# Four modulation units move to TensorE and the third piece is added whole

## The chip, the cores and the metric

The kernel runs on one core of a Trainium2 chip. The metric is the device time of one execution in microseconds. The kernel before takes 972.9 us (median of 3 runs, 971.4 to 973.92).

## The reference

Two layers of a decoder trunk on 256 tokens of width 2048, all in float32. Each layer computes a modulation from the conditioning vector `c`, scales and shifts the normalised input with it, and multiplies the result by a wide input projection:

```
c_act = silu(c)
for l in range(DEPTH):
    mod = c_act @ ada_w[l] + ada_b[l]              # (2048) @ (2048 x 6144)
    shift, scl, gate_res = split(mod, 3)
    h = _rms(x, norm_g[l]) * (1.0 + scl) + shift   # (256 x 2048)
    z = h @ w_in                                   # first layer: 2048 x 6144
    ...                                            # pooling and attention, or sparse attention and convolution
    x = x + gate_res * ((y * silu(g)) @ w_out[l])
```

What matters here is the start of the first layer: `c_act @ ada_w[0]` for the first 4096 of its columns (scale and shift), `h`, and the first twelve blocks of 128 columns of `z`.

## The kernel before, in words

**Modulation.** The weights `ada_w` come in *units* of 128 x 1024 float32 (512 KB). Sixteen units make a *piece*, which gives 1024 values of the modulation. Four pieces (units 0 to 63) hold scale and shift of the first layer, each for four of the sixteen 128-wide chunks of `h`. VectorE adds a unit into `acc` as unit times one column of `cact` plus `acc` (`add_units`, L1242). When a piece is complete, TensorE sums `acc` over the partitions: for each of 8 blocks of 128 columns one product of the block with a column of ones, written to one column of a bank (`reduce_part`, L948). VectorE adds the bias (L1266), makes the gain (L1279) and scales `X` (L1315); ScalarE adds the shift (L535). Then `h` of the chunk is there.

**Halves.** A piece can also be added in column halves: the first 8 units hold all rows of the first 512 columns, the other 8 those of the last 512. The first two chunks of the four need only the first half. In the kernel before the third and the fourth piece go so (`halved`, `half_units`, L1259 and L1262: two adds of 128 x 512 for a unit). For the fourth piece the host has put the units in this order; for the third the load itself picks the halves out of two units (`load_halves`, L334), in rows of 2 KB instead of 4 KB.

**The wide stage.** The first twelve blocks of `z` are multiplied by TensorE at once, in twelve half banks. Their weights come in twelve *wide slabs* of 1 MB and sixteen tiles. Chunk `c` of `h` is multiplied by tiles 12c to 12c + 11 (`unsplit_chunk`, L914: twelve float32 products 128 x 128 by 128 x 256, each of which the trace shows as two records). After chunk 15 ScalarE evicts the banks (L672), and the kernel goes on slab by slab to its end.

**Order.** It is written out by hand on each engine. SP issues all loads in one queue in program order: units, and wide slabs between them. A unit's load waits until its slot is free (a ring of 12), so until the unit 12 before has been added (`ada_done`); slab i waits for TensorE to have finished slab i - 4 (`pe_half`), and all behind it in SP's queue wait too. TensorE runs the chunks in order; ahead of some stand the sums: both halves of piece 0 before chunk 0 and of piece 1 before chunk 4, then the first half of piece 2 before chunk 7 and the second before chunk 9, the first half of piece 3 before chunk 11 and the second before chunk 14. Small products with the identity (`keep_warm`, L844) fill some waits.

Of the kernel before, what the change touches and what calls it, by code (L numbers as in the profile page):

```python
# [11 lines left out]
P = 128  # L12
D_MODEL = 2048
SEQ = 256
# [25 lines left out]
PIECE = 1024  # L40
# [16 lines left out]
RING = 12  # L57
TILES = KC

# [47 lines left out]
def build(nc, xT, params, pool_w, w_slabs, ada_units, x1_dram, outT):  # L107
    ctx = ExitStack()
    with ctx:
# [3 lines left out]
        def sem(name):  # L113
            return ctx.enter_context(nc.semaphore(name))
# [70 lines left out]
        half_sum = sem("half_sum")  # L185
        mod_done = sem("mod_done")
# [55 lines left out]
        def unit_slot(n):  # L242

            return n % RING if n < FIRST else n % 4
# [71 lines left out]
        def _(sp):  # L316
            sp.sem_inc(lo_done, 4 + 2 * UNSPLIT)
            sp.sem_inc(ada_done, 4)
            sp.dma_start(par[:], params).then_inc(par_in, 16)
            def load_units(n, count, t):  # L320
                for u in range(count):
                    unit = n + u if t is None else n + u + 4 * t
                    if n >= FIRST:
                        sp.wait_ge(ada_done, unit + 1)
                    elif unit >= RING:
                        sp.wait_ge(ada_done, unit - RING + 5)
# [3 lines left out]
            def load_halves(p, first, last):  # L330
                for n in range(first, last):
                    unit, half, u = UNITS * p + n, n // 8, n % 8
                    sp.wait_ge(ada_done, unit - RING + 5)
                    sp.dma_start(unit_at(unit).rearrange("p (a n) -> p a n", a=2),  # L334
                                 ada_units[UNITS * p + 2 * u:UNITS * p + 2 * u + 2, :,
                                           PIECE // 2 * half:PIECE // 2 * (half + 1)]
                                 .rearrange("a p n -> p a n")).then_inc(ada_in[unit_slot(unit)], 16)
# [498 lines left out]
        def _(pe):  # L836
# [70 lines left out]
            def unsplit_chunk(c):  # L907

                pe.wait_ge(h_done, c + 1)
                for s in range(WIDE[0]):  # L910
                    i, k = (WIDE[0] * c + s) // TILES, (WIDE[0] * c + s) % TILES
# [167 lines left out]
            halved = (2, 3)  # L1079

            def reduce_half(p, half):
                pe.wait_ge(ada_done, UNITS * p + 8 * (half + 1) + 4 if p in halved else UNITS * (p + 1) + 4)
                if not half and p:
                    pe.wait_ge(mod_done, p)
                for j in range(4 * half, 4 * half + 4):
                    ins = reduce_part(p, j, half=True)
                if not half:
                    ins.then_inc(half_sum, 1)

            for c in range(12):  # L1090
                p = c // GROUP
                if c % GROUP == 0 and p not in halved:
                    if p:
                        warm_until(UNITS + 13, UNITS + 15)
                    else:
                        warm_until(11, 15)
                    reduce_half(p, 0)
                    reduce_half(p, 1)
                if c % GROUP == GROUP - 1 and p + 1 in halved:
                    reduce_half(p + 1, 0)  # L1100
                if c % GROUP == 1 and p in halved:
                    reduce_half(p, 1)
                unsplit_chunk(c)
# [114 lines left out]
        def _(dve):  # L1218
# [33 lines left out]
            def half_units(first, count):  # L1252
                for unit in range(first, first + count):
                    u, p, half = unit % UNITS, unit // UNITS, PIECE // 2
# [3 lines left out]
                    dve.wait_ge(ada_done, unit + 4)  # L1258
# [233 lines left out]
            add_units(UNITS, 16, None)  # L1492
# [12 lines left out]
            for j in range(6):  # L1505
                lower_h(0, j)
# [3 lines left out]
            for j in range(6, 14):  # L1510
                lower_h(0, j)
            lower_h(0, 14)
            lower_h(0, 15)
# [313 lines left out]
```

## Time and profile before

| | |
|---|---|
| median of 3 runs | 972.9 us |
| the profiled execution | 975.36 us |
| its span, first to last instruction | 973.6 us |
| TensorE busy | 941.4 us (97%) |
| VectorE busy | 822.2 us (84%) |
| ScalarE busy | 427.5 us (44%) |
| mean DMA rate | 268 GB/s |
| first eviction of the wide stage | 145.46 us into the span |

Busy times of engines overlap, so they don't add up to the span. A busy share is an average over stages: the wide stage covers the first 15% of the span and has other limits than what follows. Times of rows are microseconds from the start of the span.

### The profile page before, as it was taken

How to read it: one execution, taken by the hardware profiler on the slowest of the kernel's cores; microseconds unless marked ns; L12 is line 12 of the kernel's file. 1: busy time of each engine (PE TensorE's matmuls, PEld its weight loads, DVE VectorE, ACT ScalarE, POOL GpSimd, SP SyncE). 2: the span in 40 equal slices, each digit the busy share in tenths (PEclk: the TensorE clock that was granted, in tenths of full speed). 3: DMA queues.
4: the chain of work that ended last, by engine and by line, in shares of the span. 5: the costliest groups of instructions: out<-in, count | busy, mean ns of one | idle time of the engine just before them, and what ended most of it. 6: DMA issues, size and time to landing. Idle time of an engine off the chain costs nothing.

```text
span 973.6 us, 18573 instructions
## 1 busy us (share of the span) xinstructions
PE 941.4 (97%) x7050; PEld 906.1 (93%) x7050; DVE 822.2 (84%) x1244; ACT 427.5 (44%) x742; POOL 92.5 (9%) x100
## 2 busy tenths in 40 slices
PE   4898899999999999999999999999999999999998
PEld 4887789999999999999999999999999999998887
DVE  5887868987889879998888898999999886879963
ACT  3210116444565444434445534444556655743331
POOL 1000000010110000122200000253011100000000
PEclk9999899999999999999999999999999999999999
DMA  9999978888876888899858655544555445698962
GB/s 360 412 402 404 408 267 292 309 328 336 330 275 252 310 281 312 323 352 355 326 205 284 217 190 174 176 146 159 174 173 196 173 167 201 201 308 298 360 226 76
DMA packets 76595, 261.27 MB, mean 268 GB/s; under 512 B 8288, under 2 KB 8928, under 8 KB 74608
## 3 DMA queue, kind: packets, MB, share of 16 engines
q1 hardware_dynamic: 73680, 251.38, 71.7%
q0 software_dynamic: 2848, 8.99, 2.6%
q8 instruction: 43, 0.70, 0.3%
q14 instruction: 24, 0.20, 0.1%
HBM read 256.07 MB, written 4.19 MB: 267 GB/s over the span
## 4 chain that ended last, share of the span: by engine, by line
PE 73%; DVE 20%; DMA 3%; issue 1%; ACT 1%; SPq 0%; DVEq 0%; ACTq 0%
PE bank L857 12%; PE bank L858 12%; PE bank L859 12%; DVE wlo L1232 6%; PE bank L878 6%; DVE Y L1452 6%; PE bank L914 5%; PE bank L1001 4%; PE bank L1003 4%; PE bank L1004 4%; PE bank L876 3%; DMA ada<-ada_units 2%; PE bank L927 2%; PE bank L896 2%; PE bank L902 2%; PE bank L898 2%
## 5 line engine op out<-in xcount | busy, mean ns | idle before, releaser
L517 ACT ACTIVATE whi<-raw 128x1024 fp32r<-128x1024 f32 x258 | 272.1, 1060 | 378.6 <-PE bank L859 206.5
L1232 DVE TENSOR_TENSOR wlo<-raw,whi 128x1024 fp32r<-128x1024 f32 x258 | 313.5, 1232 | 63.5 <-ACT whi L517 62.0
L857 PE MATMUL bank<-hhi,whi 128*128 128x256 f32 x912 | 262.5, 288 | 1.7 <-ACT T L763 0.9
L858 PE MATMUL bank<-hlo,whi 128*128 128x256 f32 x912 | 258.0, 283 | 0.0
L859 PE MATMUL bank<-hhi,wlo 128*128 128x256 f32 x912 | 257.9, 283 | 0.0
L1242 DVE SCALAR_TENSOR_TENSOR acc<-ada,cact,acc 128x1024 f32<-128x1024 f32 x140 | 182.5, 1303 | 22.7 <-DMA ada<-ada_units 12.3
L857 PEld LDWEIGHTS bank<-hhi,whi 128*128 128x128 f32 x912 | 174.9, 192 | 4.5 <-issue 3.1
L858 PEld LDWEIGHTS bank<-hlo,whi 128*128 128x128 f32 x912 | 175.0, 192 | 0.1
L859 PEld LDWEIGHTS bank<-hhi,wlo 128*128 128x128 f32 x912 | 174.8, 192 | 0.0
L1001 PE MATMUL bank<-whi,hhi 128*128 128x256 f32 x512 | 146.7, 287 | 0.0
L1003 PE MATMUL bank<-whi,hlo 128*128 128x256 f32 x512 | 144.8, 283 | 0.0
L1004 PE MATMUL bank<-wlo,hhi 128*128 128x256 f32 x512 | 144.8, 283 | 0.0
L1452 DVE SCALAR_TENSOR_TENSOR Y<-U,par,Y 128x256 f32<-128x256 f32 x240 | 105.2, 504 | 0.0
L1001 PEld LDWEIGHTS bank<-whi,hhi 128*128 128x128 f32 x512 | 98.2, 192 | 0.8 <-issue 0.7
L1003 PEld LDWEIGHTS bank<-whi,hlo 128*128 128x128 f32 x512 | 98.2, 192 | 0.1
L1004 PEld LDWEIGHTS bank<-wlo,hhi 128*128 128x128 f32 x512 | 98.2, 192 | 0.0
L878 PE MATMUL bank<-both_g,whi 128*128 128x512 f32 x256 | 89.5, 398 | 0.0
L857 PE MATMUL bank<-both_g,whi 128*128 128x256 f32 x256 | 73.3, 286 | 0.3 <-DVE both_g L1353 0.3
L858 PE MATMUL bank<-both_g,whi 128*128 128x256 f32 x256 | 72.4, 283 | 0.0
L859 PE MATMUL bank<-both_g,wlo 128*128 128x256 f32 x256 | 72.4, 283 | 0.0
L876 PE MATMUL bank<-both_g,wlo 128*128 128x256 f32 x240 | 68.1, 284 | 0.0
L878 PEld LDWEIGHTS bank<-both_g,whi 128*128 128x128 f32 x256 | 47.2, 188 | 10.2
(197 smaller groups left out, 1296.4 us busy)
## 6 DMA issues: line engine op xcount, KB each, us to landing
raw<-w_slabs SPq DMA_DIRECT2D x258, 512.0 KB, 4.5
ada<-ada_units SPq DMA_DIRECT2D x152, 512.0 KB, 6.6
pre<-ada_units SPq DMA_DIRECT2D x40, 512.0 KB, 15.8
raw<-w_slabs SPq DMA_DIRECT2D x6, 1024.0 KB, 15.9
V<-w_slabs SPq DMA_DIRECT2D x3, 1024.0 KB, 17.7
Y<-w_slabs SPq DMA_DIRECT2D x3, 1024.0 KB, 15.7
X<-xT SPq DMA_DIRECT2D x2, 1024.0 KB, 10.9
x_dram<-X POOLq DMA_DIRECT2D x4, 512.0 KB, 8.2
```

The source lines that it names most:

```text
L517: act.activation(whi[:, slot], raw[:, slot], ACT.Copy).then_inc(hi_done, 1)
L857: mm(out, whi[:, s, k, :], ahi[:, c, :], start=(c == 0), stop=False)
L858: mm(out, whi[:, s, k, :], alo[:, c, :], start=False, stop=False)
L859: last = mm(out, wlo[:, s, k, :], ahi[:, c, :], start=False, stop=(c == KC - 1))
L876: mm(out[:, 0:SEQ], wlo[:, s, k, :], ghi[:, c, :], start=False, stop=False, skip_group_check=True)
L878: last = mm(out[:], whi[:, s, k, :], flat(both_g[:, c]), start=(c == 0), stop=(c == KC - 1), skip_group_check=True)
L1001: mm(out, hhi[:, c, tokens], upper, start=(c == 0 and q == 0), stop=False, skip_group_check=True)
L1003: mm(out, hlo[:, c, tokens], upper, start=False, stop=False, skip_group_check=True)
L1004: last = mm(out, hhi[:, c, tokens], lower, start=False, stop=(c == KC - 1), skip_group_check=True)
L1232: dve.tensor_tensor(wlo[:, s], raw[:, s], whi[:, s].bitcast(F32), ALU.subtract)\
L1242: dve.scalar_tensor_tensor(acc[:, p % 2, :], unit_at(first + u), cact[:, bass.ds(k, 1)], acc[:, p % 2, :], ALU.mult, ALU.add).then_inc(ada ...
L1452: ins = dve.scalar_tensor_tensor(Y[:, j, :], U[:, j, k:k + SEQ], par[:, wcol:wcol + 1], Y[:, j, :], ALU.mult, ALU.add)
```

## The change

The third piece is no longer added in halves but whole, like the first two, and its units are loaded whole. Four units (31, 47, 55 and 63, the last of pieces 1 and 2 and of each half of piece 3) are not added by VectorE: TensorE multiplies each by its column of `cact`, eight products of 128 x 128 by 128 x 1, straight into the columns of the bank in which the sum over `acc` then accumulates. They stand inside chunks 3, 7, 10 and 12 (`unsplit_chunk(c, at, between)`). The sum of piece 2 stands whole between chunks 7 and 8; the half sums of piece 3 stand inside chunks 11 and 13. A new semaphore, `pe_added`, frees the slots of TensorE's units. VectorE makes all low parts of `h` (`lower_h`) at the end.

```diff
+ON_PE = (31, 47, 55, 63)
+def added(unit):
+    return unit - sum(3 * UNITS <= u < unit < FIRST for u in ON_PE)
...
             for i, first, last in ((4, 0, 3), (5, 3, 8), (6, 8, 11), (7, 11, 13), (8, 13, 16)):
-                load_halves(2, first, last)
+                load_units(2 * UNITS + first, last - first, None)
                 load_wide(sp, i)
...
+            def add_unit(unit):
+                p, n = unit // UNITS, unit % UNITS
+                pe.wait_ge(ada_in[unit_slot(unit)], 16 * unit_uses(unit, None))
+                if p < 3:
+                    for j in range(HC):
+                        ins = mm(sums(p, j)[:, j:j + 1], unit_at(unit)[:, j * P:(j + 1) * P], cact[:, n:n + 1],
+                                 start=j == 0 or p < 2 and j == HC // 2, stop=False, skip_group_check=True)
...
+                ins.then_inc(pe_added, 1)
...
+            def reduce_third():
+                pe.wait_ge(ada_done, 3 * UNITS - 1 + 4)
+                for j in range(HC):
+                    ins = reduce_column(2, j)
+                    if j == 0:
+                        ins.then_inc(ada_done, 1)
+                    if j == HC // 2 - 1:
+                        ins.then_inc(half_sum, 1)
+                ins.then_inc(mod_sum, 1)
+                keep_warm(4, M[:, SEQ:SEQ + P])
...
-            unsplit_chunk(12)
-            unsplit_chunk(13)
-            pe.wait_ge(ada_done, UNITS * 4 + 4)
-            for j in range(4, HC):
-                reduce_part(3, j)
-            keep_warm(6, M[:, 0:P])
+            warm_until(11, 15)
+            reduce_whole(0)
+            unsplit_chunk(0)
+            unsplit_chunk(1)
+            unsplit_chunk(2)
+            unsplit_chunk(3, 10, unit_31)
+            reduce_whole(1)
+            unsplit_chunk(4)
+            unsplit_chunk(5)
+            unsplit_chunk(6)
+            unsplit_chunk(7, 9, unit_47)
+            reduce_third()
+            unsplit_chunk(8)
+            unsplit_chunk(9)
+            unsplit_chunk(10, 9, unit_55)
+            unsplit_chunk(11, 7, lambda: reduce_half(3, 0))
+            unsplit_chunk(12, 9, unit_63)
+            unsplit_chunk(13, 9, lambda: reduce_half(3, 1))
             unsplit_chunk(14)
             unsplit_chunk(15)
...
-            half_units(2 * UNITS, 8)
-            half_units(2 * UNITS + 8, 1)
-            first_half(2)
-            half_units(2 * UNITS + 9, 7)
+            add_units(2 * UNITS, 15, None)
             dve.wait_ge(acc_zero, 4)
             half_units(48, 1)
+            dve.wait_ge(mod_sum, 3)
+            first_half(2)
             second_half(2)
```

TensorE's program from the end of chunk 6 to the start of chunk 9, in the kernel before (L914 is a product of a chunk, L948 one of a sum):

```order
L914 MATMUL bank<-X,raw 128x256 [waits wide_in1]
L914 MATMUL bank<-X,raw 128x256 x3
L948 MATMUL bank<-ones,acc 128x1 [waits mod_done,ada_done]
L948 MATMUL bank<-ones,acc 128x1 x3
L914 MATMUL bank<-X,raw 128x256 [waits wide_in1,h_done]
L914 MATMUL bank<-X,raw 128x256 x11
L914 MATMUL bank<-X,V 128x256 [waits wide_in2,h_done]
L914 MATMUL bank<-X,V 128x256 x11
L948 MATMUL bank<-ones,acc 128x1 [waits ada_done]
L948 MATMUL bank<-ones,acc 128x1 x3
L914 MATMUL bank<-X,V 128x256 [waits wide_in2,h_done]
```

The same place after the change (L921 is a product of a chunk, L1091 one of unit 47, L1102 one of a sum, L849 a warming product):

```order
L921 MATMUL bank<-X,raw 128x256 [waits wide_in1]
L921 MATMUL bank<-X,raw 128x256 x3
L921 MATMUL bank<-X,raw 128x256 [waits wide_in1,h_done]
L921 MATMUL bank<-X,raw 128x256 x8
L1091 MATMUL bank<-cact,pre 128x1 [waits ada_in11,mod_done]
L1091 MATMUL bank<-cact,pre 128x1 x7
L921 MATMUL bank<-X,raw 128x256 x3
L1102 MATMUL bank<-ones,acc 128x1 [waits ada_done]
L1102 MATMUL bank<-ones,acc 128x1 x7
L849 MATMUL bank<-ident,ones 128x128 x4
L921 MATMUL bank<-X,V 128x256 [waits wide_in2,h_done]
```

The first half sum has gone from before chunk 7, the second from behind chunk 8; both now stand before chunk 8, behind the wait for unit 47 (slot 11) itself.

VectorE's program at the end of the third piece, in the kernel before (slot 11 holds unit 47, slot 0 unit 48):

```order
L1259 SCALAR_TENSOR_TENSOR acc<-pre,cact,acc 128x512 [waits ada_done,ada_in11]
L1262 SCALAR_TENSOR_TENSOR acc<-pre,cact,acc 128x512 [waits dve_seq]
L1259 SCALAR_TENSOR_TENSOR acc<-ada,cact,acc 128x512 [waits ada_done,ada_in0,acc_zero]
L1262 SCALAR_TENSOR_TENSOR acc<-ada,cact,acc 128x512 [waits dve_seq]
L1266 TENSOR_TENSOR mod<-bank,par 128x4 [waits mod_sum]
```

And after the change:

```order
L1309 SCALAR_TENSOR_TENSOR acc<-pre,cact,acc 128x1024 [waits ada_done,ada_in10]
L1328 SCALAR_TENSOR_TENSOR acc<-ada,cact,acc 128x512 [waits ada_done,ada_in0,acc_zero]
L1331 SCALAR_TENSOR_TENSOR acc<-ada,cact,acc 128x512 [waits dve_seq]
L1335 TENSOR_TENSOR mod<-bank,par 128x4 [waits half_sum,mod_sum]
L1348 SCALAR_TENSOR_TENSOR hgain<-mod,par 128x2 [waits dve_seq]
L1384 SCALAR_TENSOR_TENSOR X<-X,hgain,DS 128x256 [waits dve_seq]
L1384 SCALAR_TENSOR_TENSOR X<-X,hgain,DS 128x256
L1335 TENSOR_TENSOR mod<-bank,par 128x4 [waits mod_sum]
```

Unit 47 is gone from VectorE; the add of unit 48 now stands ahead of both halves of the third piece's scaling, where it stood ahead of the second only.

## Rows read from the trace of the kernel before

**Rows 1.** The page: busy tenths in 40 equal slices of the span.
```profile
PE   4898899999999999999999999999999999999998
DMA  9999978888876888899858655544555445698962
```

**Rows 2.** After 146 us: a window of TensorE (busy, clock, DMA share, GB/s), then its longest wait.
```profile
146.00:975.00 829.00, 819.79 (x6458) 1.00 0.71 249
...
PE bank L1038 <- DVE SP L1436: 2.9, 6, 0.9
```

**Rows 3.** The chain that ended last, wide stage: start us, us, what, records.
```profile
39.28 20.99 PE bank L914 x96
...
113.75 18.70 PE bank L914 x72
...
134.74 10.64 PE bank L914 x48
145.46 0.67 ACT U L672 x2
```

**Rows 4.** Timeline of TensorE, wide stage: start us, us, instruction, records, [idle before].
```profile
60.11 2.84 PE L844 MATMUL bank<-ident,ones 128*128 128x128 f32 x24
62.79 1.84 PE L948 MATMUL bank<-ones,acc 128*128 128x1 f32 x16
65.32 8.78 PE L914 MATMUL bank<-X,Y 128*128 128x256 f32 x32 [0.69 <-ACT X L535]
...
82.57 0.95 PE L948 MATMUL bank<-ones,acc 128*128 128x1 f32 x8
83.38 5.43 PE L914 MATMUL bank<-X,raw 128*128 128x256 f32 x24
...
96.68 1.05 PE L948 MATMUL bank<-ones,acc 128*128 128x1 f32 x8 [2.69 <-DVE acc L1262]
97.59 1.97 PE L914 MATMUL bank<-X,V 128*128 128x256 f32 x8
...
112.39 1.36 PE L948 MATMUL bank<-ones,acc 128*128 128x1 f32 x8 [4.20 <-DVE acc L1262]
```

**Rows 5.** TensorE in windows: busy, granted clock, DMA share, GB/s.
```profile
113.00:114.50 1.50, 1.50 (x6) 0.50 0.98 401
...
120.50:122.00 1.50, 1.50 (x9) 1.00 0.68 281
```

**Rows 6.** Windows of 8 us: VectorE busy, TensorE's granted clock, DMA share, GB/s.
```profile
12.00:20.00 8.00, 3.03 (x4) 1.00 1.02 416
...
76.00:84.00 8.00, 4.88 (x9) 1.00 1.03 396
...
108.00:116.00 8.00, 7.54 (x15) 0.81 1.02 412
```

**Rows 7.** Timeline of VectorE (all but the last), then the chain of 79 to 102.
```profile
40.19 11.01 DVE L1242 SCALAR_TENSOR_TENSOR acc<-pre,cact,acc 128x1024 f32<-128x1024 f32 x8
63.84 0.16 DVE L1266 TENSOR_TENSOR mod<-bank,par 128x4 f32<-128x4 f32 x1 [1.53 <-PE bank L948]
...
95.09 0.75 DVE L1259 SCALAR_TENSOR_TENSOR acc<-pre,cact,acc 128x512 f32<-128x512 f32 x1
...
99.11 0.75 DVE L1262 SCALAR_TENSOR_TENSOR acc<-ada,cact,acc 128x512 f32<-128x512 f32 x1
...
83.09 15.15 DMA ada<-ada_units
```

**Rows 8.** Issues of SP's queue: units 45 to 47, slab 8, units 48 to 51, slab 9.
```profile
75.91 5.64 SPq L334 DMA_DIRECT2D pre<-ada_units  x3
81.59 1.46 SPq L289 DMA_DIRECT2D raw<-w_slabs  x1
83.09 5.30 SPq L327 DMA_DIRECT2D ada<-ada_units  x4
...
92.41 1.80 SPq L289 DMA_DIRECT2D raw<-w_slabs  x1
```

More of the change, by code:

```diff
@@ L319, in _, with slot_free @@
             sp.dma_start(par[:], params).then_inc(par_in, 16)
+            def slot_free(unit):
+                last = unit - RING
+                if last in ON_PE:
+                    sp.wait_ge(pe_added, ON_PE.index(last) + 1)
+                elif last >= 0:
+                    sp.wait_ge(ada_done, added(last) + 5)
             def load_units(n, count, t):
@@ L324, in load_units @@
                         sp.wait_ge(ada_done, unit + 1)
-                    elif unit >= RING:
-                        sp.wait_ge(ada_done, unit - RING + 5)
+                    else:
+                        slot_free(unit)
                     sp.dma_start(unit_at(n + u), ada_units[bass.ds(unit, 1)].rearrange("a p n -> p (a n)"))\
                       .then_inc(ada_in[unit_slot(n + u)], 16)
[L330 to L337, printed above, removed]
             load_units(0, 4, None)
@@ L1076, in warm_until @@
                     keep_warm(4, O[:, SEQ:SEQ + P])
-            halved = (2, 3)
+            def add_unit(unit):
[5 more added lines that the diff above has]
+                                 start=j == 0 or p < 2 and j == HC // 2, stop=False, skip_group_check=True)
+                else:
+                    half, k = n // 8, 2 * (n % 8)
+                    for i in range(HC):
+                        j = 4 * half + i % 4
+                        ins = mm(sums(p, j)[:, j:j + 1], unit_at(unit)[:, i * P:(i + 1) * P],
+                                 cact[:, k + i // 4:k + i // 4 + 1], start=i == 0, stop=False, skip_group_check=True)
+                ins.then_inc(pe_added, 1)
@@ new lines, in reduce_column, with reduce_whole @@
+            def reduce_column(p, j):
+                return mm(sums(p, j)[:, j:j + 1], acc[:, p % 2, j * P:(j + 1) * P], ones[:, 0:1],
+                          start=p == 0 and j % (HC // 2) == 0, stop=True,
+                          skip_group_check=True)
+            def reduce_whole(p):
+                pe.wait_ge(ada_done, UNITS * (p + 1) - p + 4)
+                for j in range(HC // 2):
+                    ins = reduce_column(p, j)
+                    if p and j == 0:
+                        ins.then_inc(ada_done, 1)
+                ins.then_inc(half_sum, 1)
+                for _ in range(3):
+                    mm(M[:, SEQ:SEQ + P], ones[:], ident[:], start=False, stop=True, skip_group_check=True)
+                for j in range(HC // 2, HC):
+                    ins = reduce_column(p, j)
+                ins.then_inc(mod_sum, 1)
+                pe.wait_ge(xr_done, GROUP * p + 1)
+                keep_warm(3, O[:, SEQ:SEQ + P])
@@ L1081, in reduce_half @@
             def reduce_half(p, half):
-                pe.wait_ge(ada_done, UNITS * p + 8 * (half + 1) + 4 if p in halved else UNITS * (p + 1) + 4)
-                if not half and p:
+                last = max(u for u in range(UNITS * p + 8 * half, UNITS * p + 8 * half + 8) if u not in ON_PE)
+                pe.wait_ge(ada_done, added(last) + 5)
+                if not half:
                     pe.wait_ge(mod_done, p)
                 for j in range(4 * half, 4 * half + 4):
-                    ins = reduce_part(p, j, half=True)
@@ L1087, in reduce_half @@
[L1087 to L1103, printed above, removed]
@@ L1491, in _ @@
             dve.wait_ge(acc_zero, 2)
[L1492 removed]
+            add_units(UNITS, 15, None)
             dve.wait_ge(acc_zero, 3)
```

34 lines of the change are left out of this document (27 added, 7 removed).

## The prediction

> **What bounds the kernel now.** I read the page first. In the 40 slices TensorE is busy 9 tenths almost throughout, and the DMA line stands at 9 in the opening slices [rows 1]; so two resources can bind at the start and only one later. After 146 us TensorE is busy 819.8 of 829 us, and the longest entry in its list of waits there is 2.9 us in six pieces [rows 2]. What happens later hangs on TensorE's place in its own program, so a shift of the end of the first wide stage should reach the end of the kernel about one for one.
>
> The change touches that stage alone: 16 chunks, from 39.28 to the first eviction at 145.46 [rows 3]. One chunk is 24 records; four undisturbed ones took 20.99 us and two took 10.64 us [rows 3], thus 5.3 us each, 85 us for sixteen. The stage lasts 106 us, so 21 us of it are something else. The TensorE timeline shows where [rows 4]: 5.1 us between chunks 3 and 4 (60.2 to 65.32), 3.6 us before chunk 9 (94.0 to 97.59, of which 2.69 idle), 5.4 us before chunk 11 (108.2 to 113.6, of which 4.20 idle), 2.4 us before chunk 14, 0.8 us for a half sum before chunk 7, and two stretches in which the chunks themselves run slower. The windows show the clock at 0.50 (1.2 GHz) after the 4.20 us idle, back at 1.00 (2.4 GHz) by 120.5 [rows 5]. The three chunks from 113.75 took 18.70 us instead of 15.9 [rows 3]: the dip cost 2.8 us.
>
> Then I asked what the modulation units wait for. In the 13 windows of 8 us from 12 us to 116 us the DMA share is 1.01 to 1.05, and the rate lies between 396 and 416 GB/s [rows 6]: the transfers are at their limit, and a unit of 512 KB costs 1.28 us of queue (0.524 MB at 410 GB/s), a wide slab 2.56 us. Landings there are set by the bytes ahead, not by when a slot comes free. VectorE, busy with half-width adds (0.75 + 0.75 us, one unit per 1.64 us), still had to wait for unit 48, whose transfer landed at 98.24 [rows 7]. Between 47 and 48 in the queue lies only wide slab 8 [rows 8], so unit 47 landed about 98.24 - 1.28 - 2.56 = 94.4 (its add began at 95.09 without a wait [rows 7], which bounds it from above).
>
> **The change, part by part.**
>
> *Third piece whole.* In the kernel before, chunks 8 and 9 need only units 32 to 39; TensorE runs both half sums of the third piece at 82.57 and 96.68, so chunks 7 and 8 (83.4 to 94.0) fill the time until unit 47 is there [rows 4]. In the new program the last unit, 47, stands inside chunk 7 and the whole sum ahead of chunk 8. TensorE can't begin chunk 8 before the landing of 47.
>
> When does it get there? The first sum now holds three small warming products between its halves and three after (24 such records take 2.84 us [rows 4], so 0.7 us for each three; together they add 0.7 us to the path); unit 31 adds 8 one-column products inside chunk 3. 16 records of that form took 1.84 us at 62.79 [rows 4], and I price a unit added by TensorE at this 1.84 us. Chunk 3 ends near 60.2 + 0.7 + 1.8 = 62.8, the second sum with its warming takes 3.3 us, chunk 4 starts at 66.0 instead of 65.32. VectorE, with 15 adds of 1.38 us from 40.19 (eight took 11.01 [rows 7]), is ready at 60.9, hence no wait of its own. Three and three quarters chunks later, with or without the dip of 1.7 us that [rows 4] shows (8.78 us for 32 records, which at 5.3 us for 24 would take 7.1), TensorE stands at unit 47 at 86 to 88. It idles until 94.4: 6.5 to 8.5 us.
>
> From the landing: unit 47 1.84, three products of chunk 7 1.33, eight columns 1.84: done at 99.4. VectorE meanwhile must add unit 48 before it touches the sum; that add can't begin before 98.24 and by the row ended at 99.86 [rows 7], later than 99.4. From the start of the modulation add to TensorE's next chunk the rows give 65.32 - 63.84 = 1.48 us [rows 4, 7]. Chunk 8 starts at 101.3. Before it started at 88.6, and chunk 9 at 97.6.
>
> *The rest of the stage.* Eight chunks, 42.4 us. Units 55 and 63 on TensorE, 2 x 1.84 = 3.7 us, now in its path though both have landed. The two half sums of the fourth piece inside chunks 11 and 13: at 82.57 four columns moved the next chunk by 0.81 us [rows 4], so 1.6 us; the products left in the chunk (five, then three of 0.44 us) hide the way over VectorE and ScalarE of some 1.5 us in chunk 11 and all but 0.3 us of it in chunk 13. End at 101.3 + 42.4 + 3.7 + 1.6 + 0.3 = 149.3, against 145.4: +3.9 us. The gains of the change are in here: the 5.4 us before chunk 11 and the 2.4 us before chunk 14 are gone. They are simply less than the 9.1 us by which the work behind chunk 8 starts later (101.3 + 5.3 - 97.6 = 9.0).
>
> *VectorE.* It sheds one unit of 1.38, sixteen times 1.64 less fifteen times 1.38, and two of 1.64: 10.2 us. None of it is worth anything while landings set the pace; what it costs is the order. It stands at the first half of the fourth piece until TensorE's half sum in chunk 11, then has 1.2 us of scaling and six units of 1.64 to do: 11.9 us after that sum began. TensorE asks for them after 0.8 + 2.2 + 5.3 + 1.8 + 4.0 = 14.1 us. Two us spare. The sixteen low parts of h, 0.34 us each, now all come after, 5.5 us in the last 10.6 us of the stage, and the first slab's low half still comes ready in time.
>
> *The queue.* Unit 43 now waits for unit 31 on TensorE, done near 62.6, and in the queue it stands behind slab 6, which the end of chunk 3 releases anyway; unit 59 waits for unit 47. Wide slab 9 is now released only by the end of chunk 7, near 97.5 to 99 instead of before 92.41 [rows 8], with units 56 to 59 behind it; but units 48 to 55 are in the queue ahead, 10 us of transfers, so it doesn't run dry. Cost nothing; without that cover, some 5 us. The rearranged 2 KB loads of the third piece ran at 396 GB/s in 76 to 84, the whole ones before and after at 416 and 412 [rows 6]; whole loads may bring unit 48 up to 1.0 us earlier. I take 0.6.
>
> *The clock.* A 2.69 us idle was followed by chunks at their usual speed, a 4.20 us one by 0.50 for some 7 us [rows 4, 5]. The new idle is longer than either, so I expect the fall. Bounds: nothing; and at the other end half speed for all 5.0 us of TensorE's work between the landing and chunk 8 (sum done at 104.4, chunk 8 at 105.9, +4.6) and the same 2.8 us again in chunk 8, +7.4. I take the row: 2.8 us, less the 0.5 us that TensorE has spare on VectorE there: +2.3.
>
> The Trainium skill ("TensorE: Matmul & The Clock Gate", section on HAM oscillation) says that bursts of products between waits for a DMA put the clock down again each time. By that rule the fall is certain here; by the 2.69 us row alone it would not come, and the sum would be +3.3. Of our two idles the trace agrees with the page on one.
>
> Sum: +3.9 + 2.3 - 0.6 = +5.6 us. Against the profiled execution (975.36, its span 973.6) that is 981.0. That execution lay 2.5 us above the median of the three runs, 972.9, so I forecast 978.5.
>
> **Rivals.**
>
> *The clock stays up and the queue is quicker.* Then +3.9 - 1.0, and if a unit on TensorE costs 1.62 (twice the 0.81 us) another 0.5 less: +2.4, 975.3. For it: no slower chunk after the 2.69 us idle. Against: an idle two to three times as long.
>
> *Landings follow the slots (the other side).* If a unit lands some 15 us after its issue whatever lies ahead, as 83.09 to 98.24 shows for unit 48 [rows 7], then VectorE's 10.2 us free the slots earlier, the third piece is complete as TensorE comes to it, and nothing waits: chunk 4 at 66.0, 12 chunks 63.6, three units 5.5, the sums 3.2 with 1.5 of way: 139.8, -5.6 us, 967.3. It decides at a landing of unit 47 at or before 88. Against it: what landed by 94.4 in the windows from 60 on (34.4 us at 400 GB/s) would have to come in 28 us, at 490 GB/s, and no window has more than 416; slab 8, ahead of unit 48, stays released by chunk 6.
>
> *The queue does run dry.* Slab 9 waits for chunk 7 and slab 10 for chunk 9, both late, with the last eight units behind. If a low clock delays both, unit 62 misses chunk 13 and 3 us come on top: +8.6, 981.5. Against: the 10 us in the queue.
>
> **Chances.** Forecast 0.55, the dry queue or a longer low clock 0.20, clock up and quicker queue 0.17, landings by slots 0.08. The last is the only one that makes the kernel faster; the third ends on either side of the bound. What a measurement of this kernel can tell from no change is about 0.3%, 2.9 us, so 975.8 is the border: of the third case two thirds count as the same, with the low edge of the forecast: faster 0.08, same 0.14, slower 0.78. The range runs from 974.0, a bit under the third case, to 984.0, the upper bound of the clock (3.9 + 7.4 = 11.3 us).
>
> **What would show it.** In the profile after: an idle of 6 to 9 us of TensorE ahead of the one-column products on unit 47, released by a DMA; the DMA share at 1.0 until 116 us; chunk 8 starting at 100 to 104; no idle before chunks 11 and 14; granted clock 0.50 near 95 to 101; the first eviction at 148 to 154. I am wrong if unit 47 lands before 90, if chunk 8 starts before 98, or if TensorE finds new waits after the stage.

## The result, and the profile after

| | before | changed |
|---|---|---|
| median of 5 runs each, side by side | 972.9 us (971.4 to 973.92) | 982.16 us (981.26 to 984.68) |
| profiled execution | 975.36 | 981.26 |
| its span | 973.6 | 979.5 |
| mean granted clock over the span | 0.993 | 0.991 |
| first eviction, the end of the stage | 145.46 | 151.15 |
| from there to the end of the span | 828.1 | 828.35 |

The ratio is 1.0094, with a 95% interval of 1.0077 to 1.0110: the changed kernel is slower by 9 us. Between the two profiled executions, 5.7 us of the 5.9 us in span arise before the first eviction. This answers [rows 2] and the last line of [rows 3]. First the work of TensorE after the stage, from a window of the changed kernel (busy, clock, DMA share, GB/s):

```profile
151.15:979.50 828.35, 819.85 (x6458) 1.00 0.71 250
```

The trace has the same 6458 records of products there as before, in 828.35 us against 828.14, so in this pair the shift of the stage's end passes through unchanged. The page of the changed kernel looks almost the same as [rows 1], and that is a lesson too: a loss of 5.9 us in 979.5 is a quarter of one slice.

The timeline of TensorE answers [rows 4] (start, us, instruction, records, idle before):

```profile
59.33 1.84 PE L1091 MATMUL bank<-cact,pre 128*128 128x1 f32 x16
...
65.11 7.07 PE L921 MATMUL bank<-X,Y 128*128 128x256 f32 x32
72.02 12.68 PE L921 MATMUL bank<-X,raw 128*128 128x256 f32 x58
92.06 3.54 PE L1091 MATMUL bank<-cact,pre 128*128 128x1 f32 x16 [7.36 <-DMA pre<-ada_units]
95.46 2.91 PE L921 MATMUL bank<-X,raw 128*128 128x256 f32 x6
98.16 2.27 PE L1102 MATMUL bank<-ones,acc 128*128 128x1 f32 x16
100.29 1.14 PE L849 MATMUL bank<-ident,ones 128*128 128x128 f32 x8
101.94 8.86 PE L921 MATMUL bank<-X,V 128*128 128x256 f32 x32 [0.51 <-ACT X L540]
110.64 7.07 PE L921 MATMUL bank<-X,Y 128*128 128x256 f32 x32
...
124.08 0.95 PE L1102 MATMUL bank<-ones,acc 128*128 128x1 f32 x8
...
137.98 0.95 PE L1102 MATMUL bank<-ones,acc 128*128 128x1 f32 x8
```

TensorE stands at unit 47 from 84.7 on and is released by its landing, 7.36 us later. Eight one-column products, sixteen records, which took 1.84 us for unit 31, then take 3.54. Chunk 8 starts at 101.94 (88.6 before), and the 32 records from there take 8.86 us where those at 110.64 take 7.07. The half sums at 124.08 and 137.98 have no idle time ahead of them. The windows answer [rows 5] (busy, clock, DMA share, GB/s):

```profile
89.00:90.50 1.50, 0.00 (x0) 0.50 1.05 426
...
96.50:98.00 1.50, 1.50 (x5) 0.50 1.02 407
...
99.50:101.00 1.50, 1.50 (x15) 1.00 1.01 404
...
102.50:104.00 1.50, 1.50 (x5) 0.50 1.04 429
...
110.00:111.50 1.50, 1.50 (x8) 1.00 0.32 128
...
125.00:126.50 1.50, 1.50 (x9) 1.00 0.00 0
```

The clock fell to 0.50 (1.2 GHz) while TensorE was still idle, so the work that the landing released began at the low level. It came back to 1.00 (2.4 GHz) near 99 and fell again from 102.5 to some 106, inside chunk 8. The last two rows show the queue at a third of its rate, and then empty.

VectorE's timeline answers [rows 7]:

```profile
89.40 2.67 DVE L1309 SCALAR_TENSOR_TENSOR acc<-pre,cact,acc 128x1024 f32<-128x1024 f32 x2 [2.37 <-DMA pre<-ada_units]
98.72 0.75 DVE L1328 SCALAR_TENSOR_TENSOR acc<-ada,cact,acc 128x512 f32<-128x512 f32 x1 [6.64 <-PE bank L1102]
...
100.46 0.16 DVE L1335 TENSOR_TENSOR mod<-bank,par 128x4 f32<-128x4 f32 x1 [0.20 <-PE bank L1102]
...
125.06 0.16 DVE L1335 TENSOR_TENSOR mod<-bank,par 128x4 f32<-128x4 f32 x1 [10.84 <-PE bank L1102]
...
138.97 0.16 DVE L1335 TENSOR_TENSOR mod<-bank,par 128x4 f32<-128x4 f32 x1 [2.96 <-PE bank L1102]
```

Unit 48's half add at 98.72 waits 6.64 us for L1102: the first column of the third piece's sum, which hands on the turn for unit 47. Unit 48 itself had landed at 95.70 (below). The prediction had the add wait for that landing only. SP's queue answers [rows 8]; these are slabs 9, 10 and 11:

```profile
98.40 0.33 SPq L296 DMA_DIRECT2D raw<-w_slabs  x1
...
110.83 0.33 SPq L296 DMA_DIRECT2D V<-w_slabs  x1
...
117.74 0.33 SPq L296 DMA_DIRECT2D Y<-w_slabs  x1
```

Last the chain of waits (start, us). It holds the landing and, behind it, TensorE, but for the way over VectorE and ScalarE before chunk 8 (1.5 us) and inside chunk 13:

```profile
74.58 17.34 DMA pre<-ada_units
...
101.94 16.20 PE bank L921 x66
...
151.15 0.67 ACT U L677 x2
```

### The profile page after: what moved, and what is told of

It reads as the page before. It is cut to its first block, busy times and chain, and to the rows that moved or that the text cites. A ratio compares the mean times of both kernels' runs of the same rounds, so it can differ in the third digit from the quotient of the medians.

```text
span 979.5 us, 18671 instructions
## 1 busy us (share of the span) xinstructions
PE 948.0 (97%) x7110; PEld 913.4 (93%) x7110; DVE 813.7 (83%) x1222; ACT 427.6 (44%) x742; POOL 95.0 (10%) x100
## 4 chain that ended last, share of the span: by engine, by line
PE 73%; DVE 20%; DMA 3%; issue 2%; ACT 1%; SPq 0%; DVEq 0%; ACTq 0%
PE bank L862 12%; PE bank L863 12%; PE bank L864 12%; PE bank L921 7%; DVE wlo L1299 7%; PE bank L883 6%; DVE Y L1521 6%; PE bank L1008 4%; PE bank L1010 4%; PE bank L1011 4%; PE bank L881 3%; DVE acc L1309 2%; PE bank L934 2%; DMA pre<-ada_units 2%; DMA X<-xT 1%
## 5 line engine op out<-in xcount | busy, mean ns | idle before, releaser
L1309 DVE SCALAR_TENSOR_TENSOR acc<-ada,cact,acc 128x1024 f32<-128x1024 f32 x144 | 189.8, 1318 | 19.2 <-DMA ada<-ada_units 8.2
L883 PEld LDWEIGHTS bank<-both_g,whi 128*128 128x128 f32 x256 | 47.2, 188 | 10.4 <-DVE X L1437 0.3
## 6 DMA issues: line engine op xcount, KB each, us to landing
X<-xT SPq DMA_DIRECT2D x2, 1024.0 KB, 10.4
```

The lines of the kernel that those rows point to most:

```text
L883: last = mm(out[:], whi[:, s, k, :], flat(both_g[:, c]), start=(c == 0), stop=(c == KC - 1), skip_group_check=True)
L1309: dve.scalar_tensor_tensor(acc[:, p % 2, :], unit_at(first + u), cact[:, bass.ds(k, 1)], acc[:, p % 2, :], ALU.mult, ALU.add).then_inc(ada ...
```

## The experiments

My theory after the result: the order is what costs. The third piece whole makes chunk 8 wait for the landing of unit 47 (theory A of the expectations); rivals put the loss on the one-column products, on the queue or on the clock. Medians are of 6 or 12 runs; ratios are against the kernel before, run beside each (median 972.8, 973.03 or 973.58 over the three sets). One of e4's six runs took 2383.53 us and is not in its ratio; the median of the other five is 980.06. First eviction and span are from one profiled execution of each kernel.

| run | median | ratio, 95% interval | first eviction | span |
|---|---|---|---|---|
| e1 third in halves | 974.82 | 1.0009 (0.9995 to 1.0022) | 143.64 | 974.5 |
| e2 third whole only | 978.73 | 1.0056 (1.0036 to 1.0077) | 146.32 | 975.7 |
| e3 unit 47 by VectorE | 979.08 | 1.0056 (1.0036 to 1.0077) | 147.68 | 976.3 |
| e4 warm in the wait | 980.11 | 1.0065 (1.0041 to 1.0090) | 149.23 | 978.4 |
| e5 before, 4 KB rows | 971.62 | 0.9984 (0.9969 to 0.9999) | 141.23 | 970.4 |
| e6 halves, 4 KB rows | 972.92 | 0.9992 (0.9978 to 1.0007) | 145.09 | 974.3 |
| e8 no unit on TensorE | 977.87 | 1.0040 (1.0026 to 1.0053) | 147.92 | 977.3 |
| e9 e5 and the fourth piece | 972.93 | 1.0001 (0.9985 to 1.0017) | 139.92 | 969.6 |
| e10 slab 7 behind unit 47 | 980.01 | 1.0064 (1.0043 to 1.0086) | 149.05 | 978.4 |
| e11 slabs 4 to 8 quartered | 971.72 | 0.9976 (0.9961 to 0.9992) | 138.88 | 968.9 |
| e12 e9, other queue order | 971.51 | 0.9969 (0.9956 to 0.9982) | 140.63 | 972.2 |
| e13 e8, warm in the wait | 977.09 | 1.0036 (1.0019 to 1.0053) | 144.71 | 973.1 |

Two readings of the table need care. The profiled execution lay between 2.2 us below (e13) and 3.2 us above (e6) the median of its kernel, so a difference of 2 or 3 us between two first evictions isn't yet one between two kernels. And the span less the first eviction, 828.14 before and 828.35 changed, is 828.4 to 831.6 in the experiments: the stage of e1 ended 1.8 us earlier than that of before, yet its span is 0.9 us longer, and e12 spends 3.4 us more behind the stage than before. Why isn't shown.

**e1: the changed kernel with the third piece in halves again.**

```
-ON_PE = (31, 47, 55, 63)
+ON_PE = (31, 55, 63)
-                load_units(2 * UNITS + first, last - first, None)
+                load_halves(2, first, last)
             unsplit_chunk(6)
-            unsplit_chunk(7, 9, unit_47)
-            reduce_third()
+            reduce_half(2, 0)
+            unsplit_chunk(7)
             unsplit_chunk(8)
+            reduce_half(2, 1)
             unsplit_chunk(9)
```

> The changed kernel with the third piece as before: loaded and added in column halves, half sums ahead of chunks 7 and 9, unit 47 by VectorE. Units 31, 55 and 63 stay on TensorE, the half sums of the fourth piece stay inside chunks 11 and 13. Theory A (the whole third piece costs the time, because chunk 8 waits for the landing of units 47 and 48, and the idle there lowers the clock): chunk 9 starts near 97.6 as before, then 7 chunks of 5.3 us, two units of 1.7 and two half sums of 0.8: the stage ends near 140.0 against 145.5 of before and 151.2 of the changed kernel; the kernel takes 966 to 969 us, faster than before. Theory B (the products of units on TensorE are the cost): they are all but one still there, so it stays 4 us or more slower than before, 977 or more.

```profile
59.52 1.92 PE L1100 MATMUL bank<-cact,pre 128*128 128x1 f32 x16 [0.89 <-DMA pre<-ada_units]
...
97.82 1.05 PE L1111 MATMUL bank<-ones,acc 128*128 128x1 f32 x8 [2.21 <-DVE acc L1341]
...
121.73 1.92 PE L1106 MATMUL bank<-cact,ada 128*128 128x1 f32 x16 [0.65 <-DMA ada<-ada_units]
123.51 4.96 PE L930 MATMUL bank<-X,raw 128*128 128x256 f32 x14
```

974.82: 7.3 of the 9.3 us come back, which names the main step, but no theory's number was met: A had 966 to 969. The wait before chunk 11 is gone as A has it. In the profile the rest of the miss is in other places: chunk 9 starts at 98.74, not 97.6; the stage ends at 143.64, not 140.0; and behind it come 2.7 us more than before. TensorE now meets two units before they have landed, unit 31 (0.89 us) and unit 63 (0.65 us), and the products behind both run at a low clock: 14 records in 4.96 us behind unit 63 (at 5.3 us for 24 they would take 3.1).

**e2: the kernel before with only the third piece whole, all of it added by VectorE.**

```
-                load_halves(2, first, last)
+                load_units(2 * UNITS + first, last - first, None)
-            halved = (2, 3)
+            halved = (3,)
-            half_units(2 * UNITS, 8)
-            half_units(2 * UNITS + 8, 1)
-            first_half(2)
-            half_units(2 * UNITS + 9, 7)
+            add_units(2 * UNITS, 16, None)
             dve.wait_ge(acc_zero, 4)
             half_units(48, 1)
+            dve.wait_ge(mod_sum, 3)
+            first_half(2)
```

> The kernel before with the third piece alone changed: whole units, added whole by VectorE (16 of them), one whole sum ahead of chunk 8, unit 48 added ahead of both halves of the scaling. No unit on TensorE, the fourth piece as before. Theory A: TensorE idles from 86 to 88 until unit 47 has landed (92) and been added (93.4), chunk 8 starts at 99 to 101, low clock after the idle; the stage ends at 148 to 151, the kernel takes 976 to 979 us. Theory B: without units on TensorE no loss, 973 or less.

```profile
93.38 3.57 PE L948 MATMUL bank<-ones,acc 128*128 128x1 f32 x16 [4.63 <-DVE acc L1242]
...
98.58 9.67 PE L914 MATMUL bank<-X,V 128*128 128x256 f32 x32 [1.62 <-ACT X L535]
```

978.73, as expected, +5.9 us. This one part alone makes the kernel slower, with no product on a unit in TensorE's program. That rests on the medians. The profiled stage ended at 146.32, before the 148 to 151 that I expected and only 0.9 us behind that of before: chunk 8 starts 10 us later, but the 4.20 us of idle time before chunk 11 and the dip behind it, which the profile of before has, aren't there.

**e3: the changed kernel, unit 47 added by VectorE** (ON_PE without 47, chunk 7 undivided, the sum waiting for sixteen adds).

> The changed kernel with unit 47 added by VectorE; units 31, 55 and 63 stay on TensorE. In the changed kernel TensorE multiplied unit 47 in 3.5 us at the low clock after its landing at 91.9, and VectorE could not start unit 48 before. If that serial step is a cost of its own, chunk 8 starts 2 to 3 us earlier (near 99) and the kernel takes 979 to 980 against 982. If the wait for the landing alone counts, it stays at 981 to 982.

```profile
93.60 3.57 PE L1102 MATMUL bank<-ones,acc 128*128 128x1 f32 x16 [7.57 <-DVE acc L1307]
...
98.88 8.45 PE L921 MATMUL bank<-X,V 128*128 128x256 f32 x32
```

979.08, 3.1 us below the changed kernel, as expected. VectorE adds the unit in 1.28 us, all of chunk 7 runs before the wait, and chunk 8 starts at 98.88 instead of 101.94. On TensorE the unit costs 3.54 us at the low clock, with three products of chunk 7 still to come behind it.

**e8: no unit on TensorE at all** (ON_PE empty; the sums wait for all sixteen adds).

> The changed kernel with all 64 units added by VectorE: third piece whole, fourth in halves with its half sums inside chunks 11 and 13. Theory A (the whole third piece is most of the loss, 7 of 9 us by e1; the units on TensorE the rest): units 47, 55 and 63 leave TensorE's path, 1.7 us each and 3.5 for unit 47 at the low clock, VectorE adds up to 1.3 us of wait in chunk 13: 976 to 978, still slower than before. If the units on TensorE were the main loss: 973 or less.

```profile
93.68 3.57 PE L1102 MATMUL bank<-ones,acc 128*128 128x1 f32 x16 [8.14 <-DVE acc L1303]
...
133.34 1.26 PE L1102 MATMUL bank<-ones,acc 128*128 128x1 f32 x8 [1.34 <-DVE acc L1325]
```

977.87, as expected: against e3, units 31, 55 and 63 cost 1.2 us together, with intervals that overlap, where their durations add up to 5.5 us. By the profiles unit 31 costs nothing, since both kernels start the third sum near 93.6, when unit 47 has landed and been added; and without units 55 and 63 TensorE waits 1.34 us in chunk 13, with slower products behind it (22 records in 6.47 us against 5.37). e8 is 1.1 us nearer to its kernel before than e2. It has the half sums inside the chunks, where e2 has not, but also other warming products and the low parts of `h` at the end; which of them counts isn't shown, and these intervals overlap too.

**e4: the changed kernel with 25 warming products in the wait.**

```
                 pe.wait_ge(mod_done, 2)
+                for u, count in ((42, 4), (43, 5), (44, 12), (45, 4)):
+                    pe.wait_ge(ada_done, u + 5)
+                    keep_warm(count, M[:, SEQ:SEQ + P])
                 add_unit(47)
```

> The changed kernel with 25 small warming products between the landings of units 42 to 45, while TensorE waits for unit 47 in chunk 7. If the low clock after the idle is a cost of its own (3.0 us on the way to chunk 8 and 1.8 us in chunk 8 by the profile of the changed kernel), the granted clock stays at 1.00 from 84 to 106, unit 47 takes 1.7 instead of 3.5 us, chunk 8 starts near 99.0 instead of 101.9, and the stage ends near 146.4: 4.8 us less than the changed kernel, 977 us against 982. If the wait for the landing alone sets chunk 8, nothing moves: 981 to 982.

TensorE, then VectorE:

```profile
93.30 1.95 PE L1091 MATMUL bank<-cact,pre 128*128 128x1 f32 x16
...
96.48 1.84 PE L1102 MATMUL bank<-ones,acc 128*128 128x1 f32 x16
...
100.02 8.86 PE L921 MATMUL bank<-X,V 128*128 128x256 f32 x32 [0.69 <-ACT X L540]
```

```profile
97.10 0.75 DVE L1331 SCALAR_TENSOR_TENSOR acc<-ada,cact,acc 128x512 f32<-128x512 f32 x1 [3.70 <-DMA ada<-ada_units]
```

980.11, a gain of 2.1 us (the intervals overlap a little), which misses the expectation of 4.8. Up to chunk 8 the clock stays up, but chunk 8 starts only 1.9 us earlier. In this execution all landings came 1.3 us later, that of unit 47 at 93.25 instead of 91.92; from there to chunk 8 it is 6.8 us instead of 10.0. And VectorE must now wait until 97.10 for unit 48, which it adds before it may touch the sum. The low clock had hidden a second landing behind the first. The dip inside chunk 8 is still there (8.86 us).

**e13: e8 with the same warming and four more behind unit 46's add.**

> The kernel of e8 (977.9: third piece whole, no unit on TensorE, half sums inside chunks) with 29 small warming products in the wait for units 42 to 46, as in e4. What is left then is the wait for the landing alone. The profile of e8 shows the sum at 3.57 us instead of 1.84 and the first 32 records of chunk 8 on at 9.27 instead of 7.07 us: up to 4 us. e4 got 2.1 us from the same step. I expect 975 to 976; if the clock cost nothing there, 978.

```profile
89.31 6.64 PE L849 MATMUL bank<-ident,ones 128*128 128x128 f32 x58
95.79 1.84 PE L1102 MATMUL bank<-ones,acc 128*128 128x1 f32 x16
...
99.14 7.17 PE L921 MATMUL bank<-X,V 128*128 128x256 f32 x32 [0.51 <-ACT X L540]
```

977.09, above the 975 to 976 expected. In the profile neither of the two dips shows (one near 64 does, ahead of the wait for the landing), and the stage ends 3.2 us earlier than e8's. The medians differ by 0.8 us only (intervals 1.0019 to 1.0053 and 1.0026 to 1.0053), so warming is not shown to help beyond single executions. Chunk 8 did not start earlier than e8's 98.96.

**e10: slab 7 behind unit 47 in the queue.**

```
-            for i, first, last in ((4, 0, 3), (5, 3, 8), (6, 8, 11), (7, 11, 13), (8, 13, 16)):
+            for i, first, last in ((4, 0, 3), (5, 3, 8), (6, 8, 11)):
                 load_units(2 * UNITS + first, last - first, None)
                 load_wide(sp, i)
+            load_units(2 * UNITS + 11, 5, None)
+            load_wide(sp, 7)
+            load_wide(sp, 8)
```

> The changed kernel with one thing moved in the queue: wide slab 7 (1 MB, needed in chunk 9) is issued behind unit 47 instead of ahead of unit 43; slab 8 follows it as before. If the landing of unit 47 is set by the bytes ahead of it, it lands 2.56 us earlier (89.3 instead of 91.9), unit 48 lands where it did (near 96), chunk 8 starts 1 to 2.5 us earlier, and the kernel takes 980 to 981 against 982.2. If the landing follows the slots or the issue, nothing moves.

```profile
60.48 2.00 PE L1094 MATMUL bank<-cact,pre 128*128 128x1 f32 x16 [0.40 <-DMA pre<-ada_units]
...
70.16 8.19 PE L924 MATMUL bank<-X,Y 128*128 128x256 f32 x32
...
90.88 1.92 PE L1094 MATMUL bank<-cact,pre 128*128 128x1 f32 x16
...
99.99 8.71 PE L924 MATMUL bank<-X,V 128*128 128x256 f32 x32 [3.11 <-ACT X L543]
```

980.01, as expected. The idle time before unit 47 is gone, and most of the loss stays. In this execution TensorE was late, though: a short wait for unit 31 was followed by ten us at 0.50 (62 to 72), and chunk 4 started at 70.16 instead of 65.11. Unit 47 landed at 90.74, as TensorE came to it. The landings of this execution were 1.3 us late like those of e4; counted from the landing of unit 42, unit 47 came after 8.9 us instead of 11.4, that is 2.5 us sooner, which is the 2.56 us of the slab no longer ahead of it. Unit 48 landed at 96.98 as in e4, chunk 8 waited for that, 3.11 us, and started 2 us before the changed kernel's. An earlier unit 47 by itself moves the wait to unit 48.

**e11: slabs 4 to 8 loaded to a quarter.** It leaves out three quarters of the weights of five slabs, so the products read old values; the instructions of the engines are unchanged.

```
+            part = 4 if 4 <= i <= 8 else TILES
-            eng.dma_start(wide_tiles(i), w_slabs[i:i + 1].rearrange("a p k n -> p (a k) n"))\
+            eng.dma_start(wide_tiles(i)[:, 0:part, :], w_slabs[i:i + 1, :, 0:part, :].rearrange("a p k n -> p (a k) n"))\
```

> The changed kernel with only the first quarter of wide slabs 4 to 8 loaded (the chunks multiply what an earlier slab left in the other tiles): 7.7 us of transfers less ahead of unit 47 and 9.6 us less ahead of unit 48; every instruction of the engines stays. If the landings are the bound, unit 47 is there when TensorE comes to it at 84.7, VectorE's adds (86.5) come next, chunk 8 starts near 91 instead of 102, no idle and no low clock: the stage ends near 140 instead of 151, the kernel takes 971 to 973. If TensorE's own added products or VectorE's order were the bound, it stays above 978.

```profile
84.83 1.92 PE L1092 MATMUL bank<-cact,pre 128*128 128x1 f32 x16 [0.50 <-DMA pre<-ada_units]
...
91.34 7.17 PE L922 MATMUL bank<-X,V 128*128 128x256 f32 x32 [0.51 <-ACT X L541]
```

The same program with fewer bytes: unit 47 lands at 84.70 and costs 1.92 us, chunk 8 starts 10.6 us earlier, no low clock, and 971.72, that is 10.4 us below the changed kernel. Landings are the cause, shown by taking bytes away. It is the strongest run of the study. It also shows how little the change is worth even without that wait: 0.24% (0.08% to 0.39%) below the kernel before, which still loads its slabs whole.

**e5: the kernel before, its third piece laid out by the host so that a load has rows of 4 KB, not two of 2 KB.**

```
-                load_halves(2, first, last)
+                load_units(2 * UNITS + first, last - first, None)
+    pieces[2] = two_rows(pieces[2])
     pieces[3] = two_rows(pieces[3])
```

> The kernel before with the units of the third piece put in order of halves by the host, so that each is loaded in rows of 4 KB instead of 2 KB; nothing else. The changed kernel got unit 47 at 91.9 where I had put 94.4. If the row length sets the rate (396 to 399 GB/s against 411 to 416): units 47 and 48 land 2 us earlier than before, TensorE's idle before chunk 9 falls from 2.7 to about 1 us. VectorE sets chunk 11 all the same, so the kernel gains 0 to 2 us: 971 to 973. If the rate was due to something else, unit 48 lands at 98 as before.

```profile
76.00:84.00 8.00, 8.00 (x41) 7.07 (x39) 5.53 (x8) 0.00 (x0) 0.00 (x0) 1.00 1.03 419
```

419 GB/s where [rows 6] has 396, and 971.62: 0.16% faster, an interval that just leaves out 1. Unit 47 landed at 93.29 and unit 48 at 97.06, 1.2 us earlier than before and not 2, and the idle time before chunk 9 was 2.20 us and not 1. Counted from the landing of slab 3, the third piece and its four slabs took 30.6 us instead of 32.9.

**e6: e1 with the same layout.**

> The kernel of e1 (third piece in halves, units 31, 55, 63 on TensorE, half sums inside chunks 11 and 13) with the third piece ordered by the host, rows of 4 KB. In e1 TensorE waited for the landing of unit 63 at 121.7, which my 140 us for the end of the stage had left out. If the queue is what is left, unit 63 lands 1 to 2 us earlier and the kernel takes 972 to 973.5 against 974.8 of e1. If the low clock around the one-column products is what is left, nothing moves, or the gain is lost again in dips: 974 to 975.

972.92, 1.9 us below e1, as expected. With the column halves back, the rest of the change is not shown to be worth anything: beside e5, which has the same rows without it, e6 is 1.3 us slower, with intervals that overlap.

**e9: e5 with the change's treatment of the fourth piece** (units 55 and 63 on TensorE, half sums inside chunks 11 and 13), and eight warming products before the third piece's second half sum.

> The kernel before with three things: third piece ordered by the host (rows of 4 KB), fourth piece as in the change (units 55 and 63 on TensorE, half sums inside chunks 11 and 13), and eight small warming products in the wait before chunk 9. First and second piece as before. It keeps what the change has of good and drops the whole third piece and unit 31. TensorE loses its waits before chunk 11 (1 to 4 us) and chunk 14 (2.4 us) and pays 3.4 us for two units; the last landing near 120 allows an end of the stage at 140. I expect 968 to 971 us, faster than both kernels; if the low clock eats it, 972.

```profile
104.52 1.92 PE L1097 MATMUL bank<-cact,pre 128*128 128x1 f32 x16 [0.28 <-DMA pre<-ada_units]
106.30 6.25 PE L921 MATMUL bank<-X,raw 128*128 128x256 f32 x20
...
119.70 1.92 PE L1097 MATMUL bank<-cact,ada 128*128 128x1 f32 x16 [0.22 <-DMA ada<-ada_units]
```

Its profiled execution ended its stage at 139.92, but the median of 972.93 is no gain over e5; 968 to 971 was missed. Waits before chunks 11 and 14 became short waits at the landings of units 55 and 63, and the first of them brought a dip: 20 records in 6.25 us, where 5.3 us for 24 makes 4.4. Where the other executions lose their time isn't known, since only one of each kernel is profiled.

**e12: e9 with slab 7 behind unit 47 and slab 10 behind unit 63.**

```
+            load_units(2 * UNITS + 11, 5, None)
+            load_wide(sp, 7)
+            load_wide(sp, 8)
+            load_units(3 * UNITS, 8, None)
+            load_wide(sp, 9)
+            load_units(3 * UNITS + 8, 8, None)
+            load_wide(sp, 10)
+            load_wide(sp, 11)
```

> The kernel of e9 (972.9) with the queue rearranged: slab 7 behind unit 47, slab 10 behind unit 63. In e9 TensorE waited 0.3 and 0.2 us for the landings of units 55 and 63, and VectorE's half-width adds set chunk 9. With unit 63 2.6 us earlier its landing drops out, with unit 47 earlier VectorE is the bound: 0.5 to 1.5 us less, 971.4 to 972.4. If slab 7 or 10 comes late for chunk 9 or 13, it is no faster, 973 or more.

971.51, 0.31% faster than before (0.18% to 0.44%), the best of the study and faster than both kernels. The wait for unit 63 is gone as expected, but the one for unit 55 grew to 1.13 us, again with 20 records in 6.25 us behind it. e12 isn't told apart from e5 (971.62): what is shown is the layout with 4 KB rows plus these edits, not the share of each.

Together, as medians over the kernel before: third piece whole +5.9 (e2); half sums inside the chunks, warming and low parts of `h` -1.1 (e8 less e2); units 31, 55, 63 on TensorE +1.2 (e3 less e8); unit 47 on TensorE +3.2 (changed less e3): +9.2 us, the whole but for rounding. Each term is the step from one kernel to the next, so that they add up to the whole is no check on them, and each carries about 1 us of its own; the two in the middle are not told apart from nothing. What stands clear is e2, the larger part.

## Why the prediction was right, and where it wasn't

**Chunk 8 waits for unit 47.** Right, and shown by e2 and e11. For the kernel before, the landing was read rightly: unit 47 was issued at 79.1 and landed 15.4 us later, at 94.48 (94.4 by the prediction), 3.8 us ahead of unit 48. What was mis-sized is how much faster the whole loads are. I took 0.6 us, of 1.0 at most; unit 47 landed at 91.92, and unit 48, issued at 79.49, at 95.70: both 2.5 us earlier than before. Unit 47 of before, then unit 48 of the changed kernel:

```profile
L334 SPq DMA_DIRECT2D pre<-ada_units x1: 2474/2474/2474, 79.1 to 79.1; - x1
DMA to landing us min/median/max: 15.4/15.4/15.4
```

```profile
L341 SPq DMA_DIRECT2D ada<-ada_units x1: 432/432/432, 79.5 to 79.5; - x1
DMA to landing us min/median/max: 16.2/16.2/16.2
```

TensorE came to the unit at 84.7, not 86 to 88: the dip of 1.7 us near 65 didn't recur (7.07 us at 65.11 against 8.78 in [rows 4]), and chunk 4 started 0.9 us earlier than I had it. So both ends of the idle time moved and its length, 7.36 us, lay within 6.5 to 8.5.

**From the landing to chunk 8.** With the clock up it is 6.8 us from the landing of unit 47 (93.25 to 100.02 in e4), against 6.9 forecast (94.4 to 101.3). What I named as the bound there, unit 48's landing and add, is indeed what binds in e4; in the changed kernel itself it was the turn handed on by the first sum column, at the low clock.

**The rest of the stage.** 48.0 us forecast from chunk 8 to the end; 151.15 - 101.94 = 49.2 measured, of which 1.8 is the dip in chunk 8, so 47.4. Unit 31 took 1.84 us, the half sums 0.95, and the idle time before chunks 11 and 14 is gone. VectorE was asked for its last half at 137.98 with some 2 us to spare, as forecast.

**The clock.** The fall came, and by the profiles it cost more than the +2.3: from the landing of unit 47 to chunk 8 it took 10.0 us, and 6.8 in e4, so 3.2; and 1.8 in chunk 8, 5.0 together. The medians show 2.1 us for the part that e4 takes away. I had taken the 2.8 us of [rows 5], less slack, as one dip; there were two. I had also reasoned from two idles only, 2.69 and 4.20 us, and left out that the profile of before has a dip behind an idle of 0.69 us (8.78 us for 32 records at 65.32). The rule of the Trainium skill ("TensorE: Matmul & The Clock Gate", section on HAM oscillation), by which such waits for a DMA put the clock down, holds here, with 0.50 in the row at 89.00. Taking the fall as certain was right.

**The queue.** "Doesn't run dry" was wrong: the DMA share fell to 0.32 at 110.0 and to 0.00 at 125. "Costs nothing" was right all the same: units and slabs came in time, and TensorE waited for none of them after chunk 8. The rival of a dry queue had the event and not the price.

**The sum.** +5.6 us to the stage's end; measured +5.7 (145.46 to 151.15). That agreement is largely luck: the clock was 2.7 us dearer, the landing 1.9 us earlier than the forecast had it (93.8), and the rest of the stage 0.6 us shorter.

**From the profile to the median.** This step failed. The sum gave 981.0 for the profiled execution, and 981.26 was measured; then I took off the 2.5 us by which the profiled execution of before lay above its median, and forecast 978.5 where the median is 982.16. My sum was built up from the start of the stage and had no dip of before in it, so 981.0 already was a time of the changed kernel; the distance of one execution of before from its median says nothing of that kernel. The changed kernel's own profiled execution lay 0.9 us below its median. What the 2.5 us of before consist of stays open. They are about the size of the 2.8 us dip of [rows 3], which the change removes, and it is tempting to say that the median run of before lacks it; but the mean granted clock of that execution, 0.993, is also the middle one of the 81 further runs of before, and the 27 of them with 0.993 took from 970.7 to 977.0 us. The remaining 1.2 us lie within the spread of the changed kernel's own five runs, whose profiled one was the fastest. There the time goes with the clock: 981.26 and 981.34 us at a mean granted clock of 0.991, 982.16 and 982.32 at 0.989, 984.68 at 0.986. The median of 982.16 lies inside the range of 974.0 to 984.0, but the change is +9.3 us where +5.6 was forecast, and 2.5 of the missing 3.7 us come from this step.

**The rivals.** Landings by slots (967.3) is refuted: unit 47 landed at 91.92, not by 88, and e10 moved it by just the bytes taken from ahead of it. The clock staying up is refuted by the windows, and e4 shows what keeping it up before chunk 8 is worth: 2.1 us.

## What to carry to other kernels

Where the transfers are at their limit, an operand's half that has already landed is worth more than fewer instructions: the halves let two chunks run while the last unit was on its way. Ask of each sum what stands behind it in the same engine's program, and by when its last input can land; work added to the engine that waits lies after the wait, at whatever clock the wait has left. And a profiled execution is one draw: its distance from the median of its kernel ran from -2.2 to +3.2 us here, so it is not to be carried over to another kernel. Forecast the new kernel's time from its own sum.

## What the runs showed of the hardware

- The clock had fallen before the wait was over (0.50 at 89.0 in an idle stretch that began at 84.7). Eight one-column float32 products, sixteen records, took 1.84 us at 2.4 GHz and 3.54 to 3.57 at 1.2 GHz. With small products in the wait the clock was 1.00 from 84 to 100 in e4, and from 89 to 107 in e13.
- A second dip came in chunk 8, 3 us after the clock was back, behind an idle of 0.51 us. It also came in e4 (0.69 us) and e10 (3.11 us), and not in e13 and e11 (0.51 us each). Dips also followed the products on unit 31 in e10 (0.40 us wait), e1 (0.89 us) and e6 (0.86 us), on unit 63 in e1 (0.65 us) and on unit 55 in e9 (0.28 us) and e12 (1.13 us), and none followed those on unit 31 in e3 (0.27 us), on unit 63 in e9 (0.22 us) or on any unit in the changed kernel that was there in time. Idle times of 2.69 us (before) and 2.21 us (e1) before chunk 9 were followed by full speed, and of 2.20 us by a low clock in e5 and e6 (8 records in 3.48 and 3.76 us, against 1.97). What sets them is open.
- A transfer of 512 KB in rows of 2 KB moved at 396 to 399 GB/s where rows of 4 KB moved at 411 to 419, under the same load: in the windows from 60 to 84, before against e5 and the changed kernel. From the landing of slab 3 to that of unit 47, 12.6 MB further on, it was 32.9 us before and 31.8 in e1 (2 KB), and 30.4 to 30.6 us in the changed kernel and in e2, e3, e4, e5, e6, e8, e9 and e13 (4 KB).
- With the queue full, transfers landed one behind the other in bytes: unit 48 landed 3.8 us behind unit 47, with 1.6 MB from one landing to the other, in the kernel before, the changed one and e4.
